# Attention units of the second block begin by a table, and the copy of turned probabilities stands ahead of the weight copy

## The reference, cut to what matters

```python
p = h @ w_in                                    # pool_v, pool_g, q, k, v, attn_g
q = rope(rms(q)); k = concat(kc, rope(rms(k)))  # kc, vc: of the context rows
s = einsum('bqhnd,bkhnd->bhnqk', q, k) * 64 ** -0.5
p_ = softmax(s); a = p_[:, :, 0] - lam * p_[:, :, 1]
o = einsum('bhqk,bkhe->bqhe', a, v)
attn_o = rms(o) * (1 - lam_init) * silu(attn_g)
pool_o = multiscale_pool(pool_v) * silu(pool_g)
x = x + gate * (concat(pool_o, attn_o) @ w_out)
```

## Time and profile before

| | |
|---|---|
| median of three runs | 4185.69 us |
| the profiled execution | 4181.53 us |
| its span | 4179.9 us |
| TensorE matmul busy | 3892.6 us, 93% of the span |
| VectorE, ScalarE busy | 2505.4 us (60%), 1733.9 us (41%) |
| pool gates of layer 0, attention gates of layer 0 | 2984 to 3101 us, 3260 to 3376 us (from step 4 on) |
| pool gates of layer 1, attention gates of layer 1 | 3766 to 3856 us, 3979 to 4073 us |

### The profile page before, as it was taken

One profiled execution on the slowest core, in us unless ns is written; L12 is line 12 of the kernel. 1 busy time (PEld: TensorE's weight loads), 2 busy tenths in 40 slices (PEclk: granted clock), 3 DMA queues, 4 the chain that ended last, 5 costly groups with the idle time before them and its releaser, 6 DMA issues.

```text
span 4179.9 us, 86812 instructions
## 1 busy us (share of the span) xinstructions
PE 3892.6 (93%) x36288; PEld 3305.7 (79%) x36288; DVE 2505.4 (60%) x4410; ACT 1733.9 (41%) x3145; POOL 271.2 (6%) x436
## 2 busy tenths in 40 slices
PE   6999998789989899999999999999999999898989
PEld 3778787566666699898999999878677778777778
DVE  2544678555555676587777777754543643736364
ACT  2544323433433444446444444442343432525353
POOL 0000111222222100000000000000000000000000
PEclk8999999899999999999999999999999999999999
DMA  9422666455555587474666666532222232423335
GB/s 363 146 70 70 211 212 197 132 163 172 173 171 164 188 257 236 163 242 144 212 216 209 214 210 213 175 116 91 66 76 86 61 124 95 165 91 101 102 105 178
DMA packets 288657, 666.63 MB, mean 159 GB/s; under 512 B 21072, under 2 KB 31312, under 8 KB 286496
## 3 DMA queue, kind: packets, MB, share of 16 engines
q1 hardware_dynamic: 233392, 441.74, 32.8%
q0 software_dynamic: 54896, 219.53, 16.8%
HBM read 641.26 MB, written 19.92 MB: 158 GB/s over the span
## 4 chain that ended last, share of the span: by engine, by line
PE 81%; DVE 10%; ACT 3%; issue 3%; DMA 2%; SPq 0%; POOL 0%; DVEq 0%; ACTq 0%; POOLq 0%
PE psum L851 61%; PE psum L816 2%; PE psum L1118 2%; DVE wlo L2125 1%; PE psum L1130 1%; ACT whi L1525 1%; PE psum L875 1%; PE psum L831 1%; PE psum L1043 1%; DMA ada_head<-in_w_ada 1%; PE psum L1426 1%; PE psum L1134 1%; PE psum L1157 1%; PE psum L1107 1%; DVE smx L2853 1%
## 5 line engine op out<-in xcount | busy, mean ns | idle before, releaser
L2125 DVE TENSOR_TENSOR wlo<-raw,whi 128x512 fp32r<-128x512 f32 (+3 forms) x1568 | 1054.8, 681 | 1108.9 <-ACT whi L1525 1092.6
L1525 ACT ACTIVATE whi<-raw 128x512 fp32r<-128x512 f32 (+3 forms) x1568 | 971.2, 623 | 1541.6 <-PE psum L851 1504.9
L851 PE MATMUL psum<-hhi,whi 128*128 128x512 f32 (+1 forms) x2416 | 837.5, 347 | 62.8 <-DVE wlo L2125 21.6
L851 PE MATMUL psum<-hlo,whi 128*128 128x512 f32 (+1 forms) x2416 | 817.6, 338 | 0.0
L851 PE MATMUL psum<-hhi,wlo 128*128 128x512 f32 (+1 forms) x2416 | 817.4, 338 | 0.0
L851 PEld LDWEIGHTS psum<-hhi,whi 128*128 128x128 f32 x2416 | 467.3, 193 | 161.2 <-issue 65.5
L851 PEld LDWEIGHTS psum<-hhi,wlo 128*128 128x128 f32 x2416 | 467.2, 193 | 47.9
L851 PEld LDWEIGHTS psum<-hlo,whi 128*128 128x128 f32 x2416 | 467.9, 194 | 46.8 <-issue 2.2
L851 PE MATMUL psum<-fhi,whi 128*128 128x256 f32 x1408 | 401.6, 285 | 19.7 <-DVE wlo L2125 15.3
L851 PE MATMUL psum<-flo,whi 128*128 128x256 f32 x1408 | 400.3, 284 | 0.0
L851 PE MATMUL psum<-fhi,wlo 128*128 128x256 f32 x1408 | 400.2, 284 | 0.0
(11 more groups left out here) (422 smaller groups left out, 7041.2 us busy)
## 6 DMA issues: line engine op xcount, KB each, us to landing
raw<-in_w_in SPq DMA_DIRECT2D x328, 512.0 KB, 3.8
ada_raw<-in_w_ada POOLq DMA_DIRECT2D x192, 512.0 KB, 4.4
red_raw<-in_w_adaT POOLq DMA_DIRECT2D x128, 512.0 KB, 4.4
raw<-in_w_out SPq DMA_DIRECT2D x96, 512.0 KB, 3.6
raw<-in_w_gate SPq DMA_DIRECT2D x88, 512.0 KB, 3.9
raw<-in_w_val SPq DMA_DIRECT2D x88, 512.0 KB, 4.2
raw<-in_w_down SPq DMA_DIRECT2D x88, 512.0 KB, 4.2
ada_head<-in_w_ada SPq DMA_DIRECT2D x64, 512.0 KB, 10.5
```

The source lines that it names most:

```text
L851: mm = pe.matmul(dst, l, r, start=(k == 0 and i == 0 and first), stop=(k == nch - 1 and i == 2), skip_group_check=True)
L1525: act.activation(whi[:, lc % HL, 0:width], raw[:, (lc // 2) % RAW, lc % 2, 0:width], ACT.Copy).then_inc(w_hi, 1)
L2125: dve.tensor_tensor(wlo[:, lc % HL, 0:width], raw[:, (lc // 2) % RAW, lc % 2, 0:width], whi[:, lc % HL, 0:width].bitcast(F32), ALU.subtrac ...
```

## The change

The start of each unit comes from a table, `STARTS`, in place of a formula. For layer 0 the formula gave 4, 5, 6, 7, 9, 10, 11, 12, 14, 15, 16, 17, 19, 20, 21, 22; the table gives 4, 5, 6, 7, 9, 10, 11, 12, 13, 16, 17, 18, 20, 21, 22, 23. For layer 1 it was 6, 8, ... 20 and is 4, 6, 8, 10, 12, 16, 18, 20, with V one step later after the start (5 in place of 4) and the heads' scaling in steps 1 and 3 in place of 2 and 4. Sums and spread stand one step later in both layers. On ScalarE the part with o and aT is a function of its own, `turned`, called ahead of `hi` of the same step, and at k = 15 and 31 after the SiLUs.

```diff
-        HEADS_AT = [(1, 2), (2, 4)]
-        LAG = [(0, 1, 2, 3), (0, 2, 3, 4)]
-        SUMS_AT, SPREAD_AT = [26, 25], [29, 29]
+        HEADS_AT = [(1, 2), (1, 3)]
+        LAG = [(0, 1, 2, 3), (0, 2, 3, 5)]
+        STARTS = [[4, 5, 6, 7, 9, 10, 11, 12, 13, 16, 17, 18, 20, 21, 22, 23], [4, 6, 8, 10, 12, 16, 18, 20]]
+        SUMS_AT, SPREAD_AT = [27, 26], [30, 30]
 
         def units_at(l, k, step):
 
-            first = lambda u: 4 + 5 * u // 4 if l == 0 else 6 + 2 * u
-            return [u for u in range(len(UNITS[l])) if first(u) + LAG[l][step] == k]
+            return [u for u, first in enumerate(STARTS[l]) if first + LAG[l][step] == k]
@@ ScalarE
-                def attention(it, k):
+                def turned(it, k):
 
                     for u in units_at(l, k, 3):
                         if last_of(l, u):
@@ -2064,6 +2064,9 @@
                         nk = 2 if units[u][1] < 2 else 4
                         act.wait_ge(at_pe[l], at(AT_PE[l], f"T{u}", it))
                         done(act.activation(aTs[:, u % 2, 0:nk, :], PS[6][:, 0:nk * P].rearrange("p (k q) -> p k q", q=P), ACT.Copy))
+
+                def attention(it, k):
+
                     for u in units_at(l, k, 0):
@@ ScalarE, gates
                         c = C0[f"{name}{l}"] + 16 * j
+                        if k % 16 < 15:
+                            turned(it, k)
                         hi(c, (LA + k % 16,))
...
                             act.activation(stmp[:, m, 0:T], PS[m][:, 0:T], ACT.Silu).then_inc(blk_free, 1)
+                        if k % 16 == 15:
+                            turned(it, k)
                         attention(it, k)
```

## The result

The changed kernel takes 4201.91 us (median of four runs, 4200.48 to 4202.22); the kernel before took 4185.16 in the same comparison (4182.30 to 4192.06). The recorded ratio is 1.0044, 95% interval 1.0032 to 1.0056 (the two medians by themselves give 1.0040): slower by 16.8 us. The profiled execution of it took 4201.72 us, its span is 4200.0 us.

The account below looks back on a forecast made before the run. TensorE was taken as busy nearly throughout, layer 0's 5.84 us loop almost even with its 4.3 to 5.2 us round. 16.4 - 3.5 = 12.9 on 4181.53, plus 4.2 to the median, gave 4198.6, forecast as 4198.5 us; range 4181 to 4209.

Parts of the forecast that it names:

- Layer 0: Both layer 0 gates stretches: 7.7 us lost in each, 1.0 more at the second's end, 16.4 us slower together.
- The replay through the queues: Layer 0's first gates stretch: each start is the latest of what it waits for; gave a loss of 7.7 us.
- rival (c): Layer 0: new stalls lower the clock too, two spells per stretch at 2.5 us; +10, 4208 us; chance 0.1.
- the extra 1.0 for the end of the second stretch: End of layer 0's second stretch: L2862 stands beside the last chunk, so gating and the split of `mix` come 1.0 us later.
- Layer 1: Both layer 1 gates stretches: gain between -5.4 and, with slow clock, -2.4 us; taken as -3.5 together.
- The SiLU stall: Layer 1: TensorE's wait of 3.8 us at the SiLUs stays as 3.6; a half-clock spell behind it costs 1.5 per stretch.
- a bound: Layer 1: gain of 0 if unit 7's longer wait for its difference (2.6 us) costs clock as well.
- two things: Layer 0's ScalarE order: each aT enters the loop, 5.84 becoming 6.1 to 6.3 us, and hi waits for T or V.
- Rival (a): Layer 0: the copy's place costs nothing; layer 0 gains 2.1 us twice, layer 1 5.4; 4176 us; chance 0.13.
- (b): Layer 0: same mechanism at half size, losses partly caught up; 8.2 - 5.4 = +3, 4189 us; chance 0.24.
- the bounds: Layer 0, per stretch: -2.1 us if no ScalarE wait reached TensorE, 10.1 lost if all copies and head reads went in full.

Follow-up runs that it names:

- the spread in step 29: Kernel with the new table and o and aT behind hi as before, spread moved from step 30 to 29; 4175.76 us, ratio 0.9983.
- the table alone: The changed kernel with its new table kept but o and aT put back behind hi; 4176.34 us.
- The table with the old order and the filling: New table, o and aT behind hi, plus three unused matmuls ahead of the transposes of units 4 and 7 in layer 1; 4175.67 us, ratio 0.9982.
- the sixth kernel: Changed kernel, in layer 0 head reads and copies of units 3, 11, 15 behind hi; layer 1 took 85.1 us from heads' scaling to spread.
- the fifth kernel: Changed kernel with layer 0's head reads behind hi, copies still ahead; layer 0's stretches 4.2 and 4.0 us shorter than the changed kernel's.

## Why the prediction was right, point by point

**Time.** 4198.5 forecast, 4201.9 measured, within the range of 4181 to 4209 and of the forecast's own 4192 to 4205. The sum was +12.9; the four distances give +16.8, and so do the medians: layer 0 +17.3 for 16.4, layer 1 -0.5 for -3.5. Two of the terms don't follow to the last tenth from their own figures (3108.4 less 3100.8 is 7.6, not 7.7; spread at 3849.7 for 3851.1 is 1.4, not the 1.7 used for the attention gates); nothing hangs on it.

**Layer 0.** The replay through the queues held to a tenth of a microsecond up to unit 6, and, where no spell came, to 0.3 us up to unit 15. e of unit 3, forecast 3005.00, came at 3009.77, less the 4.76 of shift 3005.01; unit 4, 3013.28 (in the text 3013.3), came at 3013.34; unit 5, 3019.5, at 3019.62. From e of unit 6 to e of unit 7, two 512-key units in a row, the second stretch took 6.11, as forecast. The loss per stretch was to be 7.7, and 8.7 in the second; it was 8.7 and 8.6. The missing 0.9 in the first is the clock. Behind the S that waited 1.5 us in step 11 it fell:

```profile
3025.45 1.81 PE psum L1455 x4
3027.26 3.89 PE psum L851 x12
```

S took 1.81 where 1.06 is usual, the chunk 3.89 for 2.95. The second stretch had the same idle time of 1.5 us there and no spell: from heads' scaling to sums it took 120.9 us, the first 121.8. The slow matmuls lost 1.7 us, of which 0.9 reached the end. That is rival (c), in small: one spell in two stretches, at 0.9, where I had priced two per stretch at 2.5 each. Of the extra 1.0 for the end of the second stretch 0.9 came: TensorE idled 6.06 us ahead of layer 0's output product, for 5.21 before, and 5.21 again with the spread in step 29.

**Layer 1.** -3.5 forecast, -0.5 measured: this is the term that was mis-sized. The start came as replayed, S of unit 0 at 3799.48, less the shift of 22.12 of this stretch 3777.4. The loop came out at 6.93 (forecast 6.90), no wait for aTs was left but 0.5. The SiLU stall I had at 3.6 of idle time with a spell behind it; TensorE idled 2.3, and no spell came there. It came behind unit 7's 2.3, which I had only named as a bound, and cost 1.5 per stretch. The sum also had no term for the two head reads, which now stand in the loop as well as the copy:

```profile
3822.41 0.69 ACT L2076 ACTIVATE pr<-psum,smx 128x512 f32<-128x512 f32 x1 [3.95 <-DVE smx L2861]
...
3823.76 0.38 ACT L2061 ACTIVATE mix<-psum 128x256 f32<-128x256 f32 x1
...
3824.28 0.61 ACT L2066 ACTIVATE aTs<-psum 128x512 f32<-128x512 f32 x1
...
3829.89 0.69 ACT L2076 ACTIVATE pr<-psum,smx 128x512 f32<-128x512 f32 x1 [3.96 <-DVE smx L2861]
```

This loop is 7.48, where the one before it is 6.93, and T of unit 7 comes 6.03 behind its e, where T of unit 6 came 5.48 behind: 0.55 twice. With the spell this is 2.6 of the 2.7 us by which the spread came later than forecast (3874.56, less 22.12 is 3852.4, for 3849.7). And the load of `xall` hung on the spread as forecast; that its time was 13.75 us and not 14.46 was luck of 0.7 in the fourth distance:

```profile
4087.08 0.68 PE psum L1494 x8
...
4090.30 13.75 DMA xall<-x_keep
```

**The order and its causes.** The prediction said the loss follows from two things: each aT enters the loop, and hi waits for TensorE. Both are shown, not each by itself. The copies ahead cost 6.3 us per stretch, the reads ahead 5.8. In the copies' 6.3 the time of the copy and the wait for T are both on the path, and their split is only estimated above; the reads bring the wait for V and their own time, and that split wasn't tested either. The rows that I had given for the strict order of ScalarE's list (hi at 3028.42 behind aT at 3027.94) don't decide it, since that aT didn't wait; the changed kernel's rows do, with hi at 3015.84 right behind an aT that had idled 3.12 us.

**Rival (a)**, that the place costs layer 0 nothing, and (b), half the size, are out: 8.6 to 8.7 per stretch. That the table alone is a gain was in the bounds (-2.1 per stretch of layer 0; measured -1.8 and -1.3).

**What is best.** The table with the old order and the filling is the fastest by its distances (-8.6). At 4175.67 us it is level with the spread in step 29 (4175.76) and the table alone (4176.34); the intervals of the three overlap.

## What to carry to other kernels

Look-ahead work that nobody waits for isn't free to stand behind a wait: what follows it in the same queue pays. Before moving a step ahead of another, write the loop from unit to unit as a sum of rows; if its length is near the bounding engine's round (5.8 against 4.3 to 5.2 us here), an operation that enters the loop comes out in full (0.28 and 0.48 us per copy here), and a wait that enters with it comes on top. And a large total of waits names the place where an engine idles, not what it would gain: when they came back (6.2 us in place of 1.4), the waits for aTs cost 1.6 us in one stretch and 0.7 in the other. When a step is moved out of the way of a wait, look in the trace whether the wait is gone or has gone to the next operation, as it did in the sixth kernel.

## What the runs showed of the hardware

Idle times of TensorE of 1.5 to 2.3 us between short busy ones were sometimes, not always, followed by a spell at half clock (0.50). The changed kernel had one behind 1.5 us in its first layer 0 stretch and none behind the same idle time in its second; in layer 1, which idles twice for 2.3 us, the fifth kernel had one per stretch and the sixth, with the same code there, two. Every gates stretch of layer 1 in the traces had at least one without the filling, and none with it. One spell cost 1.45 us in layer 1 and 0.9 in layer 0. Matmuls without use, put in the idle time, kept the clock at 1.00 there, and layer 1's stretches became shorter by 1.4 to 1.5 us, four times of four. The Trainium skill's page "TensorE: Matmul & The Clock Gate", Part 1, gives half clock as the state that follows idling; the traces agree in that each of these spells followed idle time, and show the same idle time without a spell as well.
